# Mixture-of-experts layers: 64 of 256 tokens by fetched expert rows on VectorE, the other 192 as full-precision products straight from the load ring

## The reference

```python
def peer(h, wq, keys, u_tab, v_tab):
    ...
    def block(hblk):
        q = (hblk @ wq).reshape(PEER_BLOCK, P_HEADS, 2, D_KEY_HALF)
        s = jnp.einsum('nhpd,hpkd->nhpk', q, keys).astype(jnp.float32)
        top_s, top_i = lax.top_k(s, P_TOPK)
        ...
        best_s, best_pos = lax.top_k(cand_s, P_TOPK)
        idx = jnp.take_along_axis(cand_i, best_pos, axis=-1)
        gate = jax.nn.softmax(best_s, axis=-1)
        u = u_tab[idx]
        v = v_tab[idx]
        act = jax.nn.gelu(jnp.einsum('nd,nhkd->nhk', hblk, u))
        return jnp.einsum('nhk,nhkd->nd', (gate * act).astype(v.dtype), v)
```

## Time and profile before

| | us |
|---|---|
| median of 3 runs | 2290.4 (2287.28 to 2293.27) |
| span of the profiled execution | 2285.7 |
| TensorE busy | 2231.8 (98%) |
| VectorE busy | 1866.0 (82%) |
| ScalarE busy | 1200.2 (53%) |
| GpSimd busy | 169.6 (7%) |
| transfers | 442.32 MB, mean 194 GB/s |

### The profile page before, as it was taken

The page is one execution under the profiler, slowest core; times in us unless marked ns, Lnnn a source line. Parts: engine busy times, 40 slices in busy tenths (PEclk is TensorE's granted clock), DMA queues, the critical chain, the costliest instruction groups (busy, mean ns, idle before and its releaser), DMA issues.

```text
span 2285.7 us, 34776 instructions
## 1 busy us (share of the span) xinstructions
PE 2231.8 (98%) x13446; PEld 1880.0 (82%) x13446; DVE 1866.0 (82%) x3365; ACT 1200.2 (53%) x1754; POOL 169.6 (7%) x75
## 2 busy tenths in 40 slices
...
PEclk9999999999999999999999999999999999999999
...
GB/s 287 129 201 215 201 350 121 86 119 104 190 173 187 189 178 172 172 175 174 170 175 306 336 352 238 147 185 192 186 184 174 171 172 175 175 171 223 215 236 132
DMA packets 123508, 442.32 MB, mean 194 GB/s; under 512 B 13760, under 2 KB 16832, under 8 KB 122704
## 3 DMA queue, kind: packets, MB, share of 16 engines
...
HBM read 436.88 MB, written 3.16 MB: 193 GB/s over the span
## 4 chain that ended last, share of the span: by engine, by line
PE 82%; DVE 10%; DMA 3%; ACT 3%; issue 2%; SPq 0%; ACTq 0%; DVEq 0%
PE psum L443 20%; PE psum L451 14%; PE psum L453 13%; PE psum L452 13%; PE psum L444 10%; PE psum L446 3%; PE psum L2865 3%; DVE low L2601 3%; PE psum L445 1%; DVE acc L1778 1%; DVE cv L2109 1%; DMA ring<-in_peer_v 1%; ACT cv L1399 1%; ACT spl L1098 1%; PE psum L919 1%
## 5 line engine op out<-in xcount | busy, mean ns | idle before, releaser
L2601 DVE TENSOR_TENSOR low<-ring,spl 128x1024 fp32r<-128x1024 f32 x638 | 779.4, 1228 | 256.1 <-ACT spl L1098 255.1
L1098 ACT ACTIVATE spl<-ring 128x1024 fp32r<-128x1024 f32 x702 | 735.1, 1053 | 281.2 <-DMA ring<-in_peer_u 157.8
L443 PE MATMUL psum<-hT,spl 128*128 128x512 f32 x2016 | 722.6, 397 | 3.0 <-DVE hT L1758 2.8
L444 PE MATMUL psum<-hT,low 128*128 128x256 f32 x2016 | 565.7, 281 | 0.0
L443 PEld LDWEIGHTS psum<-hT,spl 128*128 128x128 f32 x2016 | 380.6, 189 | 77.3 <-issue 3.4
L451 PE MATMUL psum<-spl,Ws 128*128 128x512 f32 x1024 | 411.6, 402 | 6.5 <-DVE Ws L2639 6.4
L453 PE MATMUL psum<-spl,Ws 128*128 128x512 f32 x1024 | 399.1, 390 | 0.0
L452 PE MATMUL psum<-low,Ws 128*128 128x512 f32 x1024 | 396.8, 388 | 0.0
L444 PEld LDWEIGHTS psum<-hT,low 128*128 128x128 f32 x2016 | 381.7, 189 | 9.7
L1707 ACT ACTIVATE Ws<-S 128x256 fp32r<-128x256 f32 x256 | 106.6, 417 | 361.8 <-PE psum L453 356.9
L2922 POOL TENSOR_TENSOR low<-ring,spl 128x1024 fp32r<-128x1024 f32 x64 | 163.1, 2550 | 1131.7 <-ACT spl L1098 1131.7
...
## 6 DMA issues: line engine op xcount, KB each, us to landing
ring<-in_peer_u SPq DMA_DIRECT2D x256, 512.0 KB, 3.5
ring<-in_peer_v SPq DMA_DIRECT2D x256, 512.0 KB, 3.6
vring<-in_ada_w SPq DMA_DIRECT2D x56, 512.0 KB, 6.0
ring<-in_w_up SPq DMA_DIRECT2D x44, 512.0 KB, 5.3
aring<-in_ada_w SPq DMA_DIRECT2D x40, 512.0 KB, 5.0
ring<-in_ab_in SPq DMA_DIRECT2D x32, 512.0 KB, 3.5
ring<-in_peer_wq SPq DMA_DIRECT2D x32, 512.0 KB, 4.3
ring<-in_w_down SPq DMA_DIRECT2D x22, 512.0 KB, 5.9
```

The lines of the kernel that those rows point to most:

```text
L443: q.matmul(b[:, :].rearrange("p (z t) -> p z t", z=2), l[0], r, start=start, stop=False)
L444: return q.matmul(b[:, 0:256], l[1], r[:, 0], start=False, stop=False)
L1098: q.activation(P.spl[:, m % SLOTS, 0:w], P.ring[:, m % SLOTS, 0:w], ACT.Copy).then_inc(*P.hi.mark(m))
L2601: q.tensor_tensor(P.low[:, n % SLOTS, 0:w], P.ring[:, n % SLOTS, 0:w], P.spl[:, n % SLOTS, 0:w].bitcast(F32), ALU.subtract).then_inc(*P.lo ...
```

## The change

64 of the 256 tokens (the first 64 of token block 0, `ROWS`) leave the dense computation. For them the rows of the chosen experts are fetched: 64 tokens x 128 experts are 64 gathers of 128 rows of 4 KB from the U table and 64 from the V table, in each layer, issued by GpSimd as indirect transfers of 512 KB into a new ring of 4 slots (`gring`, `pool_rows`). The row indices are made by VectorE at the end of the first routing (`gx`). For a U gather VectorE multiplies the rows by the token (`hrep`, which TensorE and ScalarE lay out with the token on its partition) and sums, one instruction; for a V gather it adds the weighted rows to `gacc`, one instruction (`dve_row`, `dve_sum_row`). Their places in VectorE's order are written out: 13 in the second routing, then 3, 2 and 3, one per gate round, 8 at the end of the U stage, and the last 51 spread over V tiles 48 to 119.

The other 192 tokens stay dense (`DENSE`), but without splitting: TensorE takes the tile straight from the ring as stationary operand in plain float32, 8 matmuls of 192 columns for a U tile and 8 for a V tile (its output is now turned: model width on the partitions, tokens in the columns). ScalarE's copies to `spl`, VectorE's and GpSimd's `low`, the sums of PSUM and `S`, and the splits `Ws` go away for these 256 tiles of a layer; GELU is done straight out of PSUM. Gate rounds fall from 32 to 24 per half. The routing results are turned after p = 11 and p = 25. At the end of a layer the turned output is copied from PSUM (two banks by ScalarE, two by VectorE), turned back by TensorE, and `gacc` is added there with one product for each half of the width (`pe_rows`).

The diff, cut to its core:

```diff
--- before.py
+++ after.py
@@ -173,11 +173,17 @@
 SC_AFTER = {11: ((0, 0), (0, 4), (1, 0), (1, 4)), 15: ((0, 8), (1, 8), (0, 12), (1, 12))}
 
 U_BANK = (1, 4, 6)
-
-
-def lo_on_dve(n):
-
-    return not any(T + 16 <= n < T + 80 and n % 2 == T % 2 for T in T_PEER)
+ROWS = 64
+DENSE = 256 - ROWS
+GSLOTS = 4
+GROUPS = DENSE // 8
+RT_AT = (11, 25)
+DOTS_IN_ROUTE = 13
+
+
+def native(n):
+
+    return any(T + 16 <= n < T + 272 for T in T_PEER)
...
     while P.hi_next <= min(n, T_END - 1):
         m = P.hi_next
         P.hi_next += 1
+        if native(m):
+            continue
...
     for f in range(16):
         act_hi(q, P, T + f + 2)
+        if f == 2:
+            q.wait_ge(*before[2].at(("y", 1, 1)))
+            q.activation(P.hdup[:, :, :].rearrange("p k (g t) -> p k g t", g=2),
+                         bc(P.hF[:, :, 0:ROWS].unsqueeze(2), [128, 8, 2, ROWS]), ACT.Copy).then_inc(*act.mark("hdup"))
+        if f == 3:
+            for z in range(2):
+                q.wait_ge(*pe.at(("hrep", z)))
+                q.activation(P.hrep[:, z * 512:(z + 1) * 512], P.ps[6 + z][:, :], ACT.Copy).then_inc(
+                    *act.mark(("hrep", z)))
...
+    for p in range(64):
+        act_u(q, P, l, p)
...
+    for b in (0, 2):
+        q.wait_ge(*pe.at(("yT", b)))
+        q.activation(P.hF[:, 2 * b:2 * b + 2, ROWS:256], P.ps[4 + b][:, 0:2 * DENSE].rearrange("p (m t) -> p m t", m=2),
+                     ACT.Copy).then_inc(*act.mark(("yT", b)))
...
+        *act.mark(("gelu", p)))
 
...
+def dve_row(q, P, l, s):
+
+    act, dve = P.stage(f"peer{l}")[1:]
+    row = P.gring[:, s % GSLOTS, :]
+    if s == 0:
+        for z in range(2):
+            q.wait_ge(*act.at(("hrep", z)))
+    q.wait_ge(*P.gathered[s % GSLOTS].at((l, s)))
+    q.scalar_tensor_tensor(out=row, in0=row, scalar=1.0, in1=P.hrep[:, :], op0=ALU.mult, op1=ALU.mult,
+                           accum_out=P.dots[:, s:s + 1]).then_inc(*dve.mark(("row", s)))
...
+    q.wait_ge(*P.gathered[n % GSLOTS].at((l, n)))
+    if s == 0:
+        q.tensor_scalar(P.gacc[:, :], row, w, None, ALU.mult).then_inc(*dve.mark(("row", n)))
+    else:
+        q.wait_ge(*dve.at(("row", n - 1)))
+        q.scalar_tensor_tensor(out=P.gacc[:, :], in0=row, scalar=w, in1=P.gacc[:, :], op0=ALU.mult,
+                               op1=ALU.add).then_inc(*dve.mark(("row", n)))
...
+        dve_route_top(q, P, l, tb, pe, act, dve)
+    n = dve_rows(q, P, l, DOTS_IN_ROUTE, 3)
+    dve_softmax(q, P, 1, act, dve)
+    n = dve_rows(q, P, l, n, 2)
+    dve_route_out(q, P, 1, pe, dve)
     q.wait_ge(*dve.now())
     dve_gbuild(q, P, 0, 0, pe, dve)
...
+        q.wait_ge(*dve.now())
+        dve_gbuild(q, P, *((0, r + 1) if r < GROUPS - 1 else (1, 0)), pe, dve)
+        n = dve_rows(q, P, l, n, 1)
...
+        n = dve_rows(q, P, l, n, 1)
+    left = 2 * ROWS - n
+    for j in range(2 * GROUPS, 128):
+        n = dve_rows(q, P, l, n, (min(j + 1, 120) - 2 * GROUPS) * left // (120 - 2 * GROUPS) - (n - 2 * ROWS + left))
...
+    for b in (1, 3):
+        q.wait_ge(*pe.at(("yT", b)))
+        q.tensor_copy(P.hF[:, 2 * b:2 * b + 2, ROWS:256],
+                      P.ps[4 + b][:, 0:2 * DENSE].rearrange("p (m t) -> p m t", m=2)).then_inc(*dve.mark(("yT", b)))
...
+            q.wait_ge(*act.at("hdup"))
+            for z in range(2):
+                q.wait_ge(*b4dve.at(("y", 1, z)))
+                for k in range(4):
+                    t = q.matmul(P.ps[6 + z][:, k * 128:(k + 1) * 128],
+                                 P.hdup[:, 4 * z + k, :],
+                                 P.ident[:, :], start=True, stop=True)
+                t.then_inc(*pe.mark(("hrep", z)))
...
-    for j in range(64, 125):
+    for j in range(125):
+        if j < 2 * GROUPS and j % 2 == 0:
+            pe_scatter(q, P, l, 1, j // 2)
         pe_v(q, P, l, j)
-        pe_fold(q, P, ("v", l, j))
+        if j >= 64:
+            pe_fold(q, P, ("v", l, j))
+    for b in range(4):
+        for j in range(125, 128):
+            pe_v(q, P, l, j, (b,))
+        if b >= 2:
+            pe_rows(q, P, l, b - 2, 0)
     for tb in range(2):
-        for c in range(2):
-            for j in range(125, 128):
-                pe_v(q, P, l, j, (tb,), (c,))
+        pe_rows(q, P, l, tb, 1)
...
     for d in range(2):
         n = T_PEER[l] + 16 + 2 * p + d
-        sl = pe_take(q, P, n)
+        w = pe_raw(q, P, n)
         for k in range(8):
-            t = mm3_both(q, P.ps[U_BANK[p % 3] + d], cut(sl, lambda v: v[:, k * 128:(k + 1) * 128]),
-                         P.hT[:, :, k, :], k == 0, k == 7)
+            t = q.matmul(P.ps[U_BANK[p % 3] + d][:, 0:DENSE], w[:, k * 128:(k + 1) * 128], P.hF[:, k, ROWS:256],
+                         start=k == 0, stop=k == 7)
         t.then_inc(*pe.mark(("used", n), *([("u", p)] if d else [])))
+
+
+def pe_raw(q, P, n):
+
+    q.wait_ge(*P.ld[n % SLOTS].at(n))
+    return P.ring[:, n % SLOTS, :]
...
-                q.wait_ge(*dve.at(("us", 61 + tb)))
-            t = mm3(q, P.ps[4 + 2 * tb + c][:, :], cut(both(P.Ws[:, j % 3, :, :]), lambda v: v[:, tb * 128:(tb + 1) * 128]),
-                    cut(sl, lambda v: v[:, c * 512:(c + 1) * 512]), j == 0, j == 127)
-        if tb and c:
-            t.then_inc(*pe.mark(("used", n), ("v", j), *([("y", 1, 1)] if j == 127 else [])))
+    w = pe_raw(q, P, n)
+    if j % 64 == 0:
+        q.wait_ge(*dve.at(("gm", j // 64, GROUPS - 1)))
+    for b in banks:
+        o = P.ps[4 + b][:, 0:2 * DENSE]
+        if j == 0:
+            q.wait_ge(*act.at(("gelu", 61 + b // 2)))
+            q.wait_ge(*P.set_pool.at(("sel0", l)))
+            q.matmul(o.rearrange("p (m t) -> p m t", m=2), P.zz[:, :], P.S[:, 0:2, :], start=True, stop=False)
+        for m in range(2):
+            t = q.matmul(o[:, m * DENSE:(m + 1) * DENSE], w[:, (2 * b + m) * 128:(2 * b + m + 1) * 128], P.S[:, j, :],
+                         start=False, stop=j == 127 and m == 1)
+        if b == 3:
+            t.then_inc(*pe.mark(("used", n), ("v", j), *([("yT", 3)] if j == 127 else [])))
         elif j == 127:
-            t.then_inc(*pe.mark(*[("y", tb, c) for c in chunks]))
+            t.then_inc(*pe.mark(("yT", b)))
...
+def pe_rows(q, P, l, tb, c):
+
+    pe, act, dve = P.stage(f"peer{l}")
+    o = P.ps[4 + 2 * tb + c]
+    q.wait_ge(*act.at(("yT", 2 * c)))
+    q.wait_ge(*dve.at(("yT", 2 * c + 1)))
+    if (tb, c) == (1, 0):
+        q.wait_ge(*act.at(("yT", 2)))
+    if tb == 0:
+        q.wait_ge(*dve.at(("row", 2 * ROWS - 1)))
+        q.matmul(o[:, :], P.sel[:, :], P.gacc[:, c * 512:(c + 1) * 512], start=True, stop=False)
+    for m in range(4):
+        x, y = P.hF[:, 4 * c + m, tb * 128:(tb + 1) * 128], o[:, m * 128:(m + 1) * 128]
+        if tb:
+            t = q.transpose(y, x, P.ident[:, :])
+        else:
+            t = q.matmul(y, x, P.ident[:, :], start=False, stop=m == 3)
+    t.then_inc(*pe.mark(("y", tb, c)))
...
+    q.wait_ge(*dve.at("gx"))
+    q.dma_start(P.gx[ROWS:128, 0, :], P.gx[0:ROWS, 1, :]).then_inc(*P.line("rows_moved").mark(l, by=16))
+    q.wait_ge(*P.line("rows_moved").at(l))
...
+            q.wait_ge(*dve.at(("row", n - GSLOTS)))
+        q.indirect_dma_start(out=P.gring[:, n % GSLOTS, :], out_offset=None,
+                             in_=P.A[f"peer_g{l}" if n < ROWS else f"peer_v{l}"],
+                             in_offset=bass.IndirectOffsetOnAxis(P.gx[:, 0, n % ROWS:n % ROWS + 1], 0)).then_inc(
+            *P.gathered[n % GSLOTS].mark((l, n), by=16))
...
-        q.wait_ge(*P.stage(f"peer{(s - 40) // 48}")[2].at(("ws", 63)))
+        q.wait_ge(*P.stage(f"peer{(s - 40) // 48}")[0].at(("v", 63)))
```

More of the change, by code:

```diff
@@ new lines, in __init__ @@
+        self.keys = a("keys", 12288, [128, 2048])
+        self.cand = a("cand", 14336, [128, 2048])
+        self.qT = a("qT", 16384, [128, 16, 256])
+        self.sc = a("sc", 20480, [128, 2, 16, 128])
+        self.hF = a("hF", 24576, [128, 8, 256])
+        self.hrep = a("hrep", 26624, [128, 1024])
+        self.gacc = a("gacc", 26624, [128, 1024])
+        self.hdup = a("hdup", 28672, [128, 8, 128])
+        self.gring = a("gring", 27648, [128, GSLOTS, 1024])
+        self.vals = a("vals", 31744, [128, 16, 16])
@@ L329, in __init__ @@
         self.hi = self.line("split_hi")
-        self.lo_pool = self.line("split_lo_pool")
+        self.gathered = [self.line(f"rows{i}_gathered") for i in range(GSLOTS)]
         self.lo_dve = self.line("split_lo_dve")
```

331 lines of the change are left out of this document (151 added, 180 removed).

## The result

The changed kernel takes **2236.4 us** (median of 4 runs, 2230.8 to 2237.5) against 2290.3 us before (2287.3 to 2293.3): ratio 0.9765, 95% interval 0.9751 to 0.978. It is 54 us or 2.35% faster, where 24 us or 1.1% were forecast. The sign was right and the time is inside the range, but only 1.4 us above its lower end. The profiled execution has a span of 2229.2 us, 56.5 less than before.

A forecast was written before the change was run, and what follows sets the result against it. TensorE's own work was taken as the bound. 2285.7 - 8 - 72 - 19 + 12 + 1 + 14 + 3 + 41 + 3 = 2261 us of span, runs 4.7 above: 2266 us, 1.1% faster; 8-in-10 range 2235 to 2308.

The forecast's parts named there:

- the wait in layer 0's V stage: Layer 0's second half of the V stage: 81.7 MB at 380 GB/s takes 215 us, TensorE needs 174; +41 us.
- the four windows with DMA share at 1: Layer 0's second V half before the change: 376, 374, 360, 412 GB/s, mean 380, taken as the transfer rate.
- Rival (a): Transfers bind less, 412 GB/s, and plain matmul tiles cost 2.59 us: wait 24 instead of 41, 2234 us; chance 0.14.
- Dense tiles: U and V tiles of both layers: 2.62 us each instead of 2.77 and 2.75; -72 us (ends -87 and -41).
- gate rounds: Both layers: 16 rounds fewer per layer at 0.59 us each; -19 us.
- small waits: V tiles of both layers: TensorE's waits for operands of the split go; -8 us, 6 and 2.
- Rival (d): Weight loads not hidden, plain tiles cost 2.75 us as before: 67 us more, 2333 us; chance 0.02.
- The end of a layer: Behind the last V product: VectorE's copy and four closing blocks, 9.1 us against 2.2; +14 us for both layers.
- cold restart: After layer 0's closing, TensorE stands still some 10 us before the pooling stage and its clock falls; +3 us (0 to 6).
- The gathers on the engines: Routing and U stage: VectorE's rows at 1.28 us end before TensorE needs p = 11 (704) and p = 52 (778); no wait.
- rival (c): GpSimd's indirect transfers are slow: at 5 us each VectorE's rows end 46 us late in layer 1; 2312 us, chance 0.09.
- Rival (b): Ring and gathers together get only 323 GB/s: layer 0 waits 79 us, layer 1 13; 2314 us, chance 0.12.

The follow-up runs named there:

- no_gathers: Changed kernel with only the first four gathers of a layer issued, 124 of 128 left out, all VectorE row instructions kept: 2201.4 us, ratio 0.9628.
- paced_rows: Changed kernel with VectorE waiting, before the rows at V tile j, until TensorE is done with tile j - 2: 2243.0 us, ratio 0.9812.
- early_closing: Changed kernel with two rows per gate round instead of one, and one closing block ahead of VectorE's copy of the last V bank: 2204.5 us, ratio 0.9632.
- half_rows: Changed kernel with each V-table gather bringing 64 rows instead of 128, landing on SBUF partitions 0 to 63: 2262.7 us, ratio 0.9891.

## Why the prediction was off, step by step

**The sum failed at its largest positive term, the wait in layer 0's V stage: +41, and it was 25.** The V stage without gathers' bytes takes 357.9 us (no_gathers) and with them 382.5 and 382.0, so the wait costs 24.6: TensorE's weight loads wait 22.8 us for ring tiles and its matmuls 17.7, and two windows were at clock 0.83. The step that failed is the rate. It was read as the mean of "the four windows with DMA share at 1", 376, 374, 360 and 412. But full is 1.03, not 1: the changed kernel's full windows shown above (1.02 and 1.03) hold 408 to 409 GB/s. Of the four windows only the last (1.03) was full, and it had shown 412. In the first two TensorE never waited (10.00 of 10 us), so they tell what it asked for and not what the engines can do; slices of 2 us inside the first one swing with the share:

```profile
1304.00:1306.00 2.00, 2.00 (x10) 1.65 (x9) 2.00 (x4) 0.62 (x2) 0.00 (x0) 1.00 0.92 338
...
1308.00:1310.00 2.00, 2.00 (x11) 1.63 (x10) 2.00 (x3) 0.42 (x1) 0.00 (x0) 1.00 1.01 416
```

Put into the prediction's own working, 409 GB/s gives 81.7 MB / 0.409 - 174 = 26 us. That this is so near 25 is partly luck, since the bytes were off too. From V tile 64 on, the changed kernel moved this (the second line are the gathers issued in that stretch, the last two its edges):

```profile
DMA packets 21232, 77.89 MB, mean 389 GB/s; under 512 B 2372, under 2 KB 2372, under 8 KB 21093
L3032 POOL DMA_INDIRECT gring<-in_peer_v,gx x33: 935/940/1960, 1179.0 to 1333.1; - x33
...
1170.00:1180.00 10.00, 10.00 (x64) 10.00 (x63) 3.75 (x4) 0.00 (x0) 1.00 (x1) 1.00 0.90 329
1360.00:1370.00 10.00, 10.00 (x62) 9.52 (x61) 2.77 (x3) 2.56 (x4) 0.00 (x0) 1.00 0.46 168
```

33 gathers and not 40: GpSimd issues up to four ahead of VectorE, and VectorE did only 37 of the 40 rows in there, having run ahead of its places. At 409 the 77.9 MB take 190 us, which leaves a wait of 16. But the stretch took 201, since it wasn't full at its edges, and TensorE needs 176 us for it (no_gathers), not 174. In the prediction's terms: the rate took 15 us off the 41 and the bytes 10, the edges put 10 back, and the 2 us more that TensorE needs come off again: 24. paced_rows, where VectorE can't run ahead, moved 80.3 MB in its stretch and waited 32 us. Rival (a), at 412 GB/s, said 24 us of wait and 2234 in all, with the right reason for the rate and the same luck with the bytes, and got 14 in 100.

**Dense tiles, gate rounds and small waits: -72, -19 and -8 were together some 13 us too small.** In the changed kernel's timeline rows of products stand like this, in layer 1's V stage and then in layer 0's U stage up to the first gate round (start, length of the whole row):

```profile
2199.69 8.29 PE L2955 MATMUL psum<-S,ring 128*128 128x192 f32 x50
```
```profile
804.76 5.36 PE L2913 MATMUL psum<-hF,ring 128*128 128x192 f32 x32
809.96 0.63 PE L2937 MATMUL psum<-Bb,Ab 128*128 128x64 f16 x16
```

(8.29 - 0.33) / 49 = 0.162 us each, so a tile of 16 records is 2.60 us. The prediction had 2.62, 0.164 a record. That is the bigger part of the miss. The other is the kernel before: it took 2.77 from the distance of two neighbouring tiles, where the mean of the 64 tiles up to the first gate round is (820.3 - 641.3 - 1) / 64 = 2.78, with 1 us for the turned routing results in between; after, (809.96 - 642.9 - 1) / 64 = 2.60. So a U tile gains 2.78 - 2.60 = 0.18 and not 0.15, on 128 tiles 4 us a stage. That is what the U stages gained beyond the forecast (27.5 against 23), and so did layer 1's V stage: without the gathers it is 24 us shorter than before, for 20 forecast. Layer 0's is 24 shorter too, and there 24 had been forecast, 6 of them as waits of the old split. Those 6 were too many: the earlier trace rows has only 3.8 us of idle TensorE in that half. Rival (d), weight loads not hidden, is out.

**The end of a layer: right.** +14 for both layers; behind the last V product of layer 1 it was +6.8 for 7. From V to U the changed kernel has 135.2 in one profile and 137.7 in the other, so +8 to +11 against 12. The 3 us for a cold restart may be missing there: in layer 0's closing chain TensorE waits 3.38 us at most and its clock stays at 1.00.

```profile
1372.50:1382.50 10.00, 6.36 (x51) 5.46 (x50) 9.10 (x17) 2.06 (x3) 0.00 (x0) 1.00 0.41 150
```

The earlier trace rows looked at the end of layer 1, where TensorE has nothing more to do at all; in layer 0 it turns blocks back and adds up `vacc` in between. "TensorE's turning back hides behind VectorE" was true, but only just: early_closing showed that both take 2.2 us.

**The gathers on the engines: right.** No wait in the routing that TensorE feels, as forecast: L2883 came at 705.3 and 778.4, for 704 and 778 (the first of three each time). A gather keeps GpSimd 0.94 us (median), so rival (c), which begins at 4.1 us each, had nothing for it. VectorE's rows took 1.22 and 1.28 us for the 1.28 assumed, and in no_gathers all of them together cost TensorE next to nothing. "SP, VectorE and GpSimd can't run ahead of each other by more than 4 or 5 buffers" was wrong above all in layer 1: VectorE and GpSimd were done 64 us ahead of TensorE. Its V stage is 5 us above no_gathers, for +3 forecast.

**Rival (b)**, two queues sharing the engines badly, did not come: q0 and q1 together moved 408 GB/s over 150 us, where q1 alone had moved 412 in its one full window. What would have brought it about is shown by half_rows, for another reason.

**Together.** The span lies 32 us under the forecast: 17 in layer 0's V stage, 9 in the two U stages, 4 on the way from V to U, 2 in layer 1's V stage (4 gained on tiles, 2 lost on waits). Two executions of the changed kernel differ by 4.6 us in span, so of these only the first two are safe.
